# Half-width level products in a delta net's triangular inverse, and a 64-byte shift of the arena, in a kernel of two transformer blocks

## What is computed

```python
def step(s, inp):                      # one chunk of tokens; gcum = cumsum(g)
    decay = where(tri, exp(gcum_t - gcum_s), 0)
    a = eye + where(strict, (k * beta) @ k.T * decay, 0)
    sol = triangular_solve(a, concat([v * beta, k * beta * exp(gcum)]), lower=True)
    u, w = sol[..., :dv], sol[..., dv:]
    v_new = u - w @ s
    s_new = exp(g_last) * s + (k * exp(g_last - gcum)).T @ v_new
    o = (q * exp(gcum)) @ s + (q @ k.T * decay) @ v_new
```

## Time and profile before

| | |
|---|---|
| median of 3 runs | 5103.45 us (5100.71 to 5108.52) |
| profiled execution, its own time | 5102.65 us |
| its span in the trace | 5101.1 us |
| PE busy | 4379.8 us, 86% |
| PE weight loads busy | 3732.5 us, 73% |
| DVE busy | 2899.9 us, 57% |
| ACT busy | 1532.6 us, 30% |
| mean granted PE clock | 0.929 of 2.4 GHz |

### The profile page before, as it was taken

One profiled execution on the slowest core, in us unless ns is written; L12 is line 12 of the kernel. 1 busy time (PEld: TensorE's weight loads), 2 busy tenths in 40 slices (PEclk: granted clock), 3 DMA queues, 4 the chain that ended last, 5 costly groups with the idle time before them and its releaser, 6 DMA issues.

```text
span 5101.1 us, 70606 instructions
## 1 busy us (share of the span) xinstructions
PE 4379.8 (86%) x28352; PEld 3732.5 (73%) x28352; DVE 2899.9 (57%) x6099; ACT 1532.6 (30%) x2682; POOL 0.2 (0%) x4
## 2 busy tenths in 40 slices
PE   7598897899999999998877676666888897999997
PEld 7333232889999978898667666666754697999997
DVE  4746544566566442245477777777633475655654
ACT  4211111444444332242212222222100243444442
POOL 0000000000000000000000000000000000000000
PEclk9799998999999999998888888888998999999998
DMA  5354554556565544474611111111332463655653
GB/s 176 98 164 138 157 165 138 158 150 190 184 184 187 181 119 122 122 194 132 181 43 44 44 45 48 45 50 47 89 101 63 133 203 117 186 188 180 191 184 110
DMA packets 383061, 669.57 MB, mean 131 GB/s; under 512 B 43897, under 2 KB 77402, under 8 KB 382220
## 3 DMA queue, kind: packets, MB, share of 16 engines
q1 hardware_dynamic: 327168, 595.74, 39.3%
q10 hardware_dynamic: 55564, 69.31, 4.1%
HBM read 634.87 MB, written 29.46 MB: 130 GB/s over the span
## 4 chain that ended last, share of the span: by engine, by line
PE 63%; DVE 14%; ACT 2%; issue 2%; DMA 1%; ACTq 1%; DVEq 0%
PE acc L544 13%; PE acc L545 12%; PE acc L546 12%; PE acc L586 8%; PE bank L544 2%; PE bank L545 2%; PE bank L546 2%; PE bank L1644 2%; PE bank L1635 1%; PE bank L1642 1%; PE bank L2033 1%; ACT weights_hi L508 1%; DVE arena L1490 1%; DMA arena<-s_read 1%; PE acc L1459 1%
## 5 line engine op out<-in xcount | busy, mean ns | idle before, releaser
L523 DVE TENSOR_TENSOR weights_lo<-weights_ring,weights_hi 128x512 fp32r<-128x512 f32 x1600 | 1094.2, 691 | 1037.3 <-ACT weights_hi L508 1036.2
L508 ACT ACTIVATE weights_hi<-weights_ring 128x512 fp32r<-128x512 f32 x1600 | 993.1, 629 | 1096.7 <-PE acc L546 899.5
L545 PE MATMUL acc<-arena_halves,weights_hi 128*128 128x256 f32 (+2 forms) x3136 | 924.6, 295 | 0.0
L544 PE MATMUL acc<-arena_halves,weights_lo 128*128 128x256 f32 (+1 forms) x2944 | 869.3, 295 | 20.9 <-DVE weights_lo L523 11.1
L546 PE MATMUL acc<-arena_halves,weights_hi 128*128 128x256 f32 (+1 forms) x2944 | 868.5, 295 | 0.0
L544 PE MATMUL acc<-moving_halves,weights_lo 128*128 128x256 f32 (+1 forms) x2816 | 793.8, 282 | 70.7 <-DVE weights_lo L523 69.5
L546 PE MATMUL acc<-moving_halves,weights_hi 128*128 128x256 f32 (+1 forms) x2816 | 789.1, 280 | 0.0
L545 PE MATMUL acc<-moving_halves,weights_hi 128*128 128x256 f32 x2624 | 734.0, 280 | 0.0
L545 PEld LDWEIGHTS acc<-arena_halves,weights_hi 128*128 128x128 f32 x3136 | 601.9, 192 | 12.5
L544 PEld LDWEIGHTS acc<-moving_halves,weights_lo 128*128 128x128 f32 x2816 | 536.5, 191 | 78.4 <-DVE weights_lo L523 51.4
L544 PEld LDWEIGHTS acc<-arena_halves,weights_lo 128*128 128x128 f32 x2944 | 565.2, 192 | 34.6 <-DVE weights_lo L523 12.3
(11 more groups left out here) (410 smaller groups left out, 5081.9 us busy)
## 6 DMA issues: line engine op xcount, KB each, us to landing
weights_ring<-in_w_in SPq DMA_DIRECT2D x624, 256.0 KB, 2.7
weights_ring<-in_w_ff SPq DMA_DIRECT2D x512, 256.0 KB, 3.0
weights_ring<-in_w_ada SPq DMA_DIRECT2D x384, 256.0 KB, 3.0
weights_ring<-in_w_up SPq DMA_DIRECT2D x256, 256.0 KB, 3.0
weights_ring<-in_w_down SPq DMA_DIRECT2D x256, 256.0 KB, 3.3
weights_ring<-in_w_out SPq DMA_DIRECT2D x128, 256.0 KB, 3.1
weights_ring<-in_w_branch SPq DMA_DIRECT2D x96, 256.0 KB, 3.2
s_state<-arena ACTq DMA_DIRECT2D x36, 256.0 KB, 3.0
```

The costliest lines, as they stand in the source:

```text
L508: a.activation(whi, k.slot(g.ring0 + kc), ACT.Copy).then_inc(*s.made("scalar_done", "high", n))
L523: v.tensor_tensor(wlo, k.slot(g.ring0 + kc), whi.bitcast(F32), ALU.subtract).then_inc(*s.made("vector_done", "low", n))
L544: pe.matmul(g.out[m], wlo[:, cols], xhi, start=first, stop=False, skip_group_check=g.shared)
L545: pe.matmul(g.out[m], whi[:, cols], xlo, start=False, stop=False, skip_group_check=g.shared)
```

## The change

It has two parts that are independent of each other.

**Arena.** A buffer of 16 words (64 bytes) that nothing uses is placed ahead of the arena. The arena begins at byte 140736, 64 bytes past a multiple of 128, as `moving` does. The other buffers stay.

**Levels.** The first level (6) needs no general product, since x and xt are the identity: xt becomes identity - mt at once, and one product mt.T @ identity gives what is subtracted from the identity for x. In the levels below, only those columns are made that can change: half of them, in blocks. PE takes every second block of columns as its moving operand (64 columns in place of 128) and writes them side by side; DVE subtracts them from the same columns of x or xt. In HGRN2's levels, two DVE instructions for two tiles j become one over both. The background is spread over 50 rounds in place of 56.

```diff
         self.whole = sb("whole_i32", 64, dt=I32)[:, :]
+        sb("between", 16)
         with nc.sbuf_tensor("arena_halves", [P, ARENA], F32R) as self.arena_r:
...
-        for j in range(2):
-            own(v.tensor_tensor(m0[:, j], mid[:, j], c0[:, j], ALU.subtract))
-            own(v.tensor_tensor(m1[:, j], c1[:, j], mid[:, j], ALU.subtract), *(ev("spans", level) if j else ()))
+        own(v.tensor_tensor(m0, mid, c0, ALU.subtract))
+        own(v.tensor_tensor(m1, c1, mid, ALU.subtract), *ev("spans", level))
...
-        for j in range(2):
-            own(v.tensor_tensor(m0[:, j], m0[:, j], (k0 if fwd else q0)[:, j], ALU.mult))
-            own(v.tensor_tensor(m1[:, j], m1[:, j], (q1 if fwd else k1)[:, j], ALU.mult), *(ev("level", level) if j else ()))
+        own(v.tensor_tensor(m0, m0, k0 if fwd else q0, ALU.mult))
+        own(v.tensor_tensor(m1, m1, q1 if fwd else k1, ALU.mult), *ev("level", level))
...
+def level_columns(t, level, second):
+
+    return t.rearrange("p (b two n) -> p b two n", two=2, n=P >> (level + 1))[:, :, second, :]
+
+def compact(b, level):
+    return b[:, 0:64 * NT].rearrange("p (b n) -> p b n", n=P >> (level + 1))
...
-    for level in range(6, -1, -1):
+    yield
+    pe.wait_ge(*s.at(*ev("masked", 6)))
+    for j in range(NT):
+        mm = pe.matmul(b0[:, P * j:P * j + P], mt[:, j, :], k.ident, start=True, stop=True)
+    mm.then_inc(*s.made("tensor_done", *ev("left", 6)))
+    yield
+    for level in range(5, -1, -1):
...
         if level:
             for j in range(NT):
-                pe.matmul(b0[:, P * j:P * j + P], xt[:, j, :], y[:, j, :], start=True, stop=True)
+                pe.matmul(b0[:, 64 * j:64 * j + 64], xt[:, j, :], level_columns(y[:, j, :], level, r), start=True, stop=True)
         for j in range(NT):
-            mm = pe.matmul(b1[:, P * j:P * j + P], y[:, j, :], xt[:, j, :], start=True, stop=True)
+            mm = pe.matmul(b1[:, 64 * j:64 * j + 64], y[:, j, :], level_columns(xt[:, j, :], level, 1 - r), start=True, stop=True)
...
-    own(v.tensor_copy(x, idb))
-    own(v.tensor_copy(xt, idb))
-    for level in range(6, -1, -1):
+    v.wait_ge(*own.last)
+    own(v.tensor_tensor(mt, nt, k.masks[r][:, 6, :].unsqueeze(1).broadcast_to((P, NT, P)), ALU.mult), *ev("masked", 6))
+    v.wait_ge(*own.last)
+    own(v.tensor_tensor(xt, idb, mt, ALU.subtract))
+    yield
+    yield
+    v.wait_ge(*s.at(*ev("left", 6)))
+    own(v.tensor_tensor(x, idb, tiles(b0), ALU.subtract))
+    for level in range(5, -1, -1):
...
         if level:
-            own(v.tensor_tensor(x, x, tiles(b0), ALU.subtract))
-        own(v.tensor_tensor(xt, xt, tiles(b1), ALU.subtract))
+            some = level_columns(flat(x), level, r)
+            own(v.tensor_tensor(some, some, compact(b0, level), ALU.subtract))
+        some = level_columns(flat(xt), level, 1 - r)
+        own(v.tensor_tensor(some, some, compact(b1, level), ALU.subtract))
...
-        beside(lockstep(strands), 56, background(k, head, whole_tensor))
+        beside(lockstep(strands), 50, background(k, head, whole_tensor))
```

More of the change, by code:

```diff
@@ L1838, in heads2_vector @@
         strands = [forget_vector(k, r, head) for r in range(2)] + [delta_vector(k, r, head) for r in range(2)]
-        beside(lockstep(strands), 56, background(k, head, nothing))
+        beside(lockstep(strands), 50, background(k, head, nothing))
         head_end(k, "hg", head, k.ho, k.hsq, k.p("hg_norm_w"), flat(k.hgt), k.branch[1][:, head, :], k.acc[2:4], k.acc[3])
@@ L1882, in heads2_scalar @@
         strands = [forget_scalar(k, r, head) for r in range(2)] + [delta_scalar(k, r, head) for r in range(2)]
-        beside(lockstep(strands), 56, background(k, head, whole_scalar))
+        beside(lockstep(strands), 50, background(k, head, whole_scalar))
         for name, sq in (("hg", k.hsq), ("dn", k.dzs)):
```

## The result

| | before | after |
|---|---|---|
| median of the runs | 5105.99 us (4 runs, 5100.71 to 5114.74) | 5033.4 us (4 runs, 5029.32 to 5045.52) |
| ratio, 95% interval | | 0.986, 0.9838 to 0.9882 |
| profiled execution | 5102.65 us | 5032.32 us |
| its span | 5101.1 us | 5030.9 us |
| the eight heads' windows | 1123.8 us | 1067.2 us |

The profiled executions stand 70.3 us apart, the medians 72.6; the forecast was 67.1.

The account below looks back on a forecast made before the run. PE's own pace was taken to bound the fp32r streams; in the heads, PE's work in levels and tail, and DVE where PE waits. 38.9 + 7.8 + 20.4 = 67.1 us off 5102.65 gave 5036 us, range 5000 to 5075.

Parts of the forecast that it names:

- The arena, 38.9 us for 256 columns: fp32r stages: 8640 records of 256 columns from the arena save 4.5 ns each, 38.9 us (19.9 to 57.0).
- my first rival: Arena: its new place gives nothing, since `moving` has two paces at one address; 5082 us, chance 0.20.
- The arena, 7.8 us for 512 columns: fp32r stages: 1728 records of 512 columns from the arena save 4.5 ns each, 7.8 us (0 to 11.4).
- As the loss looks like a fixed amount for each matmul: Arena, 512 columns: the step that gave them the same 4.5 ns a record as 256 columns.
- The fp32 operands of the arena, nothing: Arena's fp32 operands move too; judged by the levels' tiles, whose alternating records run at one pace: 0 us.
- The levels, 20.4 us: Heads: 3.55 + 0.8 + 0.5 - 1.5 - 0.8 = 2.55 us a head saved, 20.4 us (6 lost to 56 gained).
- DVE's part: Levels: 0.8 us a head from two copies gone at line 1635, 0.5 us at line 1650 behind the last level.
- The two losses: Each head: gaps in the tail as the background ends sooner, 1.5 us; granted clock falling behind the levels, 0.8 us.
- In a level DVE's 6.74 us lie under PE's 8.80: Levels: DVE's work is covered by PE's, so half-column subtractions and HGRN2's merged instructions save nothing there.
- The arena's new place gives nothing: Rival, arena: the 64-byte move saves nothing and only the heads gain; 5082 us, chance 0.20.
- The heads give nothing: Rival, heads: gaps in the tail eat the 32 records saved, only the arena gains; 5056 us, chance 0.10.
- The clock falls in the levels: Rival, levels: halved columns drop the granted clock, 3.3 us a stretch; 5115 us if half fall, 5193 all; chance 0.06.
- The new place is worse: Rival, arena: a record from the new place takes 6.6 ns more; 5139 us, chance 0.04.

Follow-up runs that it names:

- e1: The kernel before with only the unused 64-byte buffer added ahead of the arena, levels as before: 5091.2 us, ratio 0.9977.
- e2: The changed kernel without the 64-byte buffer, so levels changed and arena at its old place: 5053.9 us, ratio 0.9902.

## Why the prediction was right, and where its terms were off

The forecast of 5036 us against 5033.4 was right in its sum and wrong in both of its large terms: the arena gave 25.6 us less than forecast and the heads 36.2 us more. That the two errors cancel is luck; nothing in the working ties the one to the other.

**The arena, 38.9 us for 256 columns.** Right that the place acts and that the time is PE's own: e1 shows it alone. Mis-sized (whole stages here, stops counted, so some tenths of a ns over the windows' paces): with 1536 records to a stage, w_down and w_ff2 went from 120.2 to 118.1 ns, 3.2 us in each of four stages; w_in2's read saved 8.9 us in the profiled execution and 3.0 when it was run again; w_branch saved 2.7. In all 24.4 us, and 18.3 in the second execution. I had taken the middle of the two paces of `moving`; the arena gets the slow one nearly always. The reason given with the change, that the arena now lies as `moving` does, is not what acts: seen from the weights, the one lies at 64 and the other at 192, and those two places differ both with 512 columns and in how often the fast pace comes. The remark in my first rival that they share no place in 256 bytes was the right thread, and I should have given it more than a chance of the place doing nothing: it was a reason for the lower end of the term.

**The arena, 7.8 us for 512 columns.** Wrong in sign, and outside its bounds (0 to 11.4 us). "As the loss looks like a fixed amount for each matmul" is the step that failed: 1728 records went from 227.9 to 229.8 ns, 3.3 us more. The place 0, worst for 256 columns, is the best of the five for 512. Arena in all: 24.4 - 3.3 = 21.1 us (18.3 - 3.4 = 14.9 in the second execution) in place of 46.7.

**The fp32 operands of the arena, nothing.** I had looked at the levels' tiles alone. In the heads it holds (140.5 us with the arena alone, 140.6 before). Between w_in and w_glu it doesn't. That stretch, from the last start of w_in to the first of w_glu, of the kernel before, with the levels alone, and of the kernel after (time, busy time of PE, PEld, DVE, ACT and POOL):

```profile
159.40:888.90 729.50, 582.26 (x1677) 205.38 (x1676) 405.21 (x845) 109.30 (x168) 0.00 (x0) 0.91 0.47 142
160.80:890.80 730.00, 583.20 (x1677) 204.07 (x1676) 405.07 (x846) 109.28 (x168) 0.00 (x0) 0.92 0.47 142
160.20:893.40 733.20, 586.36 (x1677) 204.87 (x1675) 405.06 (x845) 109.21 (x168) 0.00 (x0) 0.91 0.47 142
```

It got 3.7 us longer in these windows (3.8 by the starts themselves), PE is busy 4.1 us longer with the same records, and DVE and ACT are not. It follows the arena's place in the other kernels too: 0.5 us longer with the arena 128 from the weights, 2.2 at 32, 3.4 at 192, 3.6 to 5.0 at 64 (6.3 with `moving` on the weights' place). Which of the fp32 products pay I have not traced. With it the arena's place comes to 11 to 17 us, around the 12.0 us that the arena alone measured.

**The levels, 20.4 us.** Measured 1123.8 - 1067.2 = 56.6 us, just past the upper bound of 56. The 32 records were right to the hundredth (3.57 us against 3.55 a head), and so was the price of narrow records: nothing. DVE's part was too small. I had credited 0.8 of the 1.6 us at line 1635, as if all of it stood ahead of the first level, where 1.1 did; 1.4 of the 1.6 went. The 0.5 us behind ACT and the 0.3 us ahead of line 1655, which I had left, went too; behind the last level 0.2 went where I took 0.5. Together with smaller gaps the rest shrank by 3.45 us a head. The two losses didn't come: not the tail's gap at 50 rounds (1.5 us; the run with 44 rounds shows it there), and not the clock's (0.8 us). Sum for each head 3.57 + 3.45 = 7.0 us, in place of 2.55.

**"In a level DVE's 6.74 us lie under PE's 8.80"** was the reason to credit half subtractions with nothing. The full-width run shows that they were worth 2.2 us a head. DVE works in order, and the mask product of the next level (line 1730) stands behind both subtractions of this one; PE's first product of that level (line 1647) waits for it, however idle DVE is elsewhere in the level. A window of a level shows 2 us of free DVE time and not where in the level it lies. The earlier trace rows had the place, with two waits at line 1635, and I read them as the first level's alone; the second, 0.5 us, was such a wait in level 1.

**The rivals.** "The arena's new place gives nothing": w_down moved in every kernel that moved the arena; it fell. It was nearer to the truth of the arena's size than the forecast, though. "The heads give nothing" fell with e2. "The clock falls in the levels" fell: the granted clock is 1.00 through levels and tail of all eight heads, and falls behind them. Here are one head's windows on either side of that fall, of the kernel after:

```profile
2838.30:2920.00 81.70, 78.00 (x578) 1.00 0.21 55
2920.20:2935.00 14.80, 1.22 (x2) 0.50 0.30 97
```

The tail ends at 2918.4 us, with the sum over `hsq`; half speed lies where PE has next to nothing to do.

"The new place is worse" fell for 256 columns and is, in small, what happened to 512.

What stays open is what in the fp32 stretch pays for the arena's place. Its 3.8 us and the terms above make the difference of the profiled executions: 56.6 + 21.1 + 2.3 us (w_out2 drew the fast pace) - 3.8 = 76.2, of 70.3; some 6 us are scattered over the rest.

## What to carry to other kernels

Where PE streams fp32r products without a gap, the start of the moving operand as seen from the stationary one, modulo 256 bytes, was worth up to 6% of the stream (113.3 against 120 ns), and the best place for 256 columns was not the best for 512: try the places, one buffer at a time, and read the spacing of starts. A sum that comes out right is no proof of its terms; one kernel for each term (here two, at once) is. When an edit shortens the engine that isn't the bound, look at what its last instruction releases, not at its busy share; and if the edit also takes work away that had covered that wait, do both together.

A version that the runs point to and that wasn't tried: the arena at a distance of 192, where its long stages drew the fast pace more often (w_ff2 twice, w_down not), with the operands of w_in2 alone at a distance of 0 or 64, where 512 columns run at 227 to 229 ns in place of 233.5 (8 to 11 us). The read of the same operands with 256 columns goes against it: 1344 records at 120 ns in place of 113.3 are 9 us at a distance of 0.

## What the runs showed of the hardware that I had not expected

- The pace of 256-column fp32r records at full clock is 120.0, 118 or 113.3 ns by the distance between the moving operand and the weights, modulo 256 bytes (117 and 119 ns at 32 and 128, one kernel each), not by the address of either: at a distance of 0 it was 120 in every stage of four kernels (two from the arena, two from `moving`), whether both buffers lay at 128 or at 192 past a multiple of 256. The Trainium skill, "TensorE: Matmul & The Clock Gate", Back-to-back issue gap, gives a rule by the width alone for a single matmul, not for a stream with its weight loads; the estimate by it is 109 ns for 256 columns, and no stage of any kernel showed it.
- The same move has opposite signs by width: 64 bytes on, 256 columns gain 2 ns and 512 columns lose 2; at 32, 128 and 192 they lose 6 to 7 (233 to 233.5 against 226.7).
- At distances of 64 and 192 a stream runs at 118 or at 113 ns as long as nothing interrupts it, and after a stop it can run at the other: seven stops in w_up gave both in one stage. 113 ns is rare at 64 and frequent at 192. What draws it the runs don't show.
- fp32 records take 111 to 112 ns with 128, with 64 and with 32 columns (the timeline after); columns read in strides, two at a time, cost nothing more.
